# New call orders of four engines around the convolution of a hybrid decoder block, and nine convolution taps from GpSimd to VectorE

## What is computed

```
h = rmsnorm(x);  a_val, a_gate, b_in = split(h @ w_in)        # 512, 512, 512 channels
u  = a_val * sigmoid(a_gate)
ya = silu(layernorm(causal_dwconv(u, 31 taps) + bias))        # 4 channel groups of 128
yb = (sliding mean over 2, 4, 8, 16 tokens - token) @ pool_w * pool_scale
x  = x + concat(ya, yb) @ w_out
h  = rmsnorm(x);  gate, val = split(h @ w_up)                 # 2816 each
x  = x + (silu(causal_dwconv(gate, 3 taps)) * val) @ w_down
out = rmsnorm(x)
```

## Time and profile before

| | us |
|---|---|
| median of three runs | 907.63 |
| lowest, highest | 907.63, 907.78 |
| profiled execution, its span | 906.6 |
| busy: PE, PEld | 888.1, 735.1 |
| busy: DVE, POOL, ACT | 705.3, 674.6, 417.9 |

### The profile page before, as it was taken

How to read it: one execution, slowest core, us unless ns; L and a number is a source line. 1 busy time by engine, 2 the same in 40 slices (tenths; PEclk the granted TensorE clock), 3 DMA queues, 4 the chain that set the end, 5 groups by cost and what they waited for, 6 DMA issues and landing times.

```text
span 906.6 us, 11217 instructions
## 1 busy us (share of the span) xinstructions
PE 888.1 (98%) x4004; PEld 735.1 (81%) x4004; DVE 705.3 (78%) x759; ACT 417.9 (46%) x641; POOL 674.6 (74%) x505
## 2 busy tenths in 40 slices
PE   7999999899999999999999999999999999999996
PEld 6888887688888888888888888888888888888875
DVE  7799999997697895876858768587685876858667
ACT  8666656763564542433424434244342433424336
POOL 3679998683179896977959779597795977959822
PEclk9999999999999999999999999999999999999999
DMA  9221011151001112111121211312112021120114
GB/s 295 99 88 47 1 47 48 46 163 47 1 8 40 58 39 90 47 59 47 43 85 41 65 47 35 93 35 70 44 39 93 27 79 36 47 93 15 37 66 186
DMA packets 62997, 57.73 MB, mean 64 GB/s; under 512 B 2170, under 2 KB 56158, under 8 KB 62942
## 3 DMA queue, kind: packets, MB, share of 16 engines
q1 hardware_dynamic: 62942, 57.01, 20.0%
HBM read 52.81 MB, written 4.19 MB: 63 GB/s over the span
## 4 chain that ended last, share of the span: by engine, by line
PE 87%; DVE 7%; ACT 2%; issue 2%; DMA 1%; SPq 0%; POOL 0%; DVEq 0%; ACTq 0%; POOLq 0%
PE slot L2298 86%; DVE slot L1657 3%; PE slot L2330 1%; DVE w_lo L1622 1%; DMA x_sb<-in_x 1%; ACT junk L963 1%; DVE slot L1952 1%; DVE act_lo L1751 0%; DVE bn L1709 0%; DVE tokens L1698 0%; PE slot L2584 0%; ACT act_hi L972 0%; ACT std L966 0%; PE slot L2418 0%; PE slot L2406 0%
## 5 line engine op out<-in xcount | busy, mean ns | idle before, releaser
L753 POOL TENSOR_TENSOR ring<-raw,ring 128x512 fp32r<-128x512 f32 x200 | 275.3, 1395 | 106.2 <-ACT ring L1163 106.2
L1163 ACT ACTIVATE ring<-raw 128x512 fp32r<-128x512 f32 x204 | 120.7, 624 | 221.6 <-POOL raw L776 101.0
L2298 PE MATMUL slot<-act_hi,ring 128*128 128x512 f32 x680 | 219.7, 389 | 0.0
L1966 DVE TENSOR_TENSOR x_sb<-x_sb,slot 128x1024 f32<-128x1024 f32 x140 | 169.2, 1215 | 59.7 <-PE slot L2298 54.6
L2298 PE MATMUL slot<-sums,ring 128*128 128x512 f32 x780 | 186.9, 389 | 0.0
L2298 PEld LDWEIGHTS slot<-sums,ring 128*128 128x128 f32 x780 | 146.4, 188 | 30.4
L2298 PEld LDWEIGHTS slot<-act_hi,ring 128*128 128x128 f32 x680 | 127.7, 188 | 26.4
L715 POOL TENSOR_TENSOR conv<-conv,prod 128x512 f32<-128x512 f32 (+9 forms) x89 | 121.8, 1389 | 22.2 <-ACT prod L1078 15.5
L2298 PE MATMUL slot<-act_lo,ring 128*128 128x512 f32 x340 | 132.3, 389 | 0.0
L776 POOL TENSOR_TENSOR raw<-raw 128x512 f32<-128x512 f32 x88 | 121.6, 1383 | 13.0 <-POOL ring L753 3.4
L1657 DVE SCALAR_TENSOR_TENSOR slot<-x_sb,chan_head,slot 128x512 f32<-128x512 f32 (+16 forms) x143 | 102.0, 740 | 2.7
(11 more groups left out here) (201 smaller groups left out, 1462.8 us busy)
## 6 DMA issues: line engine op xcount, KB each, us to landing
raw<-in_w_up SPq DMA_DIRECT2D x44, 256.0 KB, 2.9
raw<-in_w_up SPq DMA_DIRECT2D x22, 512.0 KB, 3.8
raw<-in_w_down SPq DMA_DIRECT2D x22, 512.0 KB, 3.3
x_sb<-in_x SPq DMA_DIRECT2D x12, 512.0 KB, 6.1
raw<-in_w_in SPq DMA_DIRECT2D x4, 1024.0 KB, 5.0
raw<-in_w_out SPq DMA_DIRECT2D x4, 1024.0 KB, 4.9
out<-raw SPq DMA_DIRECT2D x7, 512.0 KB, 2.6
raw<-in_w_in SPq DMA_DIRECT2D x4, 512.0 KB, 8.6
```

The source lines that it names most:

```text
L753: nc.gpsimd.tensor_tensor(block_at(n, 1), block_raw(n), block_at(n, 0).bitcast(F32), ALU.subtract).then_inc(block_lo, 1)
L1163: nc.scalar.activation(block_at(n, 0), block_raw(n), ACT.Copy).then_inc(block_hi, 1)
L1966: nc.vector.tensor_tensor(dst, dst, slot[part_slot(i, p)][:, :].rearrange("p (a n) -> p a n", a=2), ALU.add).then_inc(part_added, 1)
L2298: mm = nc.tensor.matmul(out_ap, st[s], mv[v], start=first and s == v == 0, stop=last and s == 1, skip_group_check=onto)
```

## The change

Four call lists and the tables that belong to them are put in another order between the first taps and the loop over channel pairs, and the split of the taps (`LIGHT`) is set anew: (0,1) 20 to 19, (1,0) 11 to 9, (2,0) 11 to 8, (3,0) 10 to 7, (3,1) 14 to 13, (2,1) 14 to 15. The change is described as fifteen of GpSimd's taps given to VectorE; by this table ten are given and one is taken back, and GpSimd's number falls from 89 to 80. No instruction is new in kind. ScalarE's `sqrt_table()`, a one-element activation that brings in the table for the square root, is moved from ahead of `diff_hi(0)` to far behind.

```diff
-            ("pool", 0), ("pool", 1), ("pool", 2), ("pool", 3), ("out", 0), ("out", 1), ("t2", 0), ("t2", 1),
-            ("out", 2), ("out", 3), ("ln", 1, 0), ("ln", 1, 1), ("back", 1, 0), ("back", 1, 1), ("t2", 2), ("out", 4),
+            ("pool", 0), ("pool", 1), ("pool", 2), ("pool", 3), ("out", 0), ("out", 1), ("t2", 0), ("out", 2),
+            ("t2", 1), ("out", 3), ("ln", 1, 0), ("ln", 1, 1), ("back", 1, 0), ("back", 1, 1), ("t2", 2), ("out", 4),
...
-        LIGHT = {(0, 0): 5, (0, 1): 20, (1, 0): 11, (2, 0): 11, (1, 1): 12, (3, 0): 10, (2, 1): 14, (3, 1): 14}
+        LIGHT = {(0, 0): 5, (0, 1): 19, (1, 0): 9, (1, 1): 12, (2, 0): 8, (2, 1): 15, (3, 0): 7, (3, 1): 13}
...
             out(1, 0)
+            out(0, 1)
+            pool_product(2)
             out(1, 1)
-            pool_product(2)
-            out(0, 1)
             out(1, 2)
             pool_product(3)
             out(0, 2)
-            out(2, 1)
             out(0, 3)
             out(1, 3)
+            out(2, 1)
             out(2, 3)
-            out(3, 1)
             t2(0)
...
             join(2, 1)
             join(3, 1)
             t2_lo(1)
-            x1(2)
-            x1(3)
             ln_stat(1, 0)
             ln_stat(1, 1)
```

More of the change, by code:

```diff
@@ L1377, in _ @@
[L1377 to L1386 removed]
+            product(1, 1, 9)
+            product(3, 1, 2)
+            pool_tokens_half()
+            half_hi(6, 1)
+            product(3, 0, 5)
+            product(3, 1, 3)
+            product(2, 1, 3)
@@ L1387, in _ @@
+            product(3, 0, 6)
+            product(3, 1, 1)
+            half_hi(7, 0)
+            first_tap(3, 1)
             pool_tokens(2)
-            half_hi(7, 0)
-            product(2, 1, 3)
-            product(2, 1, 2)
             pool_tokens(1)
-            half_hi(7, 1)
-            sqrt_table()
             diff_hi(0)
             ln_std(0, 0)
+            half_hi(7, 1)
+            ln_std(0, 1)
             ln_z(0, 0)
-            ln_std(0, 1)
             ln_z(0, 1)
+            pool_tokens(0)
@@ L1399, in _ @@
             ln_z(0, 2)
             ln_z(0, 3)
-            pool_tokens(0)
+            diff_hi(1)
+            half_hi(8, 0)
             ln_silu(0, 0)
             ln_silu(0, 1)
-            diff_hi(1)
+            ln_silu(0, 2)
             pool_output(0)
-            ln_silu(0, 2)
+            product(2, 1, 5)
             ln_silu(0, 3)
+            pool_output(1)
             product(1, 1, 10)
-            half_hi(8, 0)
-            pool_output(1)
             diff_hi(2)
-            product(2, 1, 5)
@@ L1473, in _ @@
             s1_high(6)
+            high(0, T3)
+            sqrt_table()
+            s3_high(6)
             s2_high(5)
-            s3_high(6)
             p1_copy(0)
@@ L2031, in _ @@
             unit_lo(5, 0)
-            taps((2, 0, 5))
+            taps((2, 0, 4))
+            taps((1, 1, 2), (2, 0, 2))
+            taps((2, 0, 2))
+            tap(1, 1)
+            taps((2, 0, 4))
+            make_u(3)
             tap(1, 1)
             tap(2, 0)
-            taps((1, 1, 2))
-            tap(2, 0)
+            unit_lo(5, 1)
+            taps((2, 0, 3))
             tap(1, 1)
-            tap(2, 0)
-            make_u(3)
-            taps((2, 0, 7))
-            tap(1, 1)
-            taps((2, 0, 2))
-            tap(1, 1)
-            join(2, 0)
-            taps((3, 0, 3))
-            unit_lo(5, 1)
-            tap(3, 0)
-            tap(1, 1)
-            taps((3, 0, 7))
-            taps((1, 1, 2))
-            taps((3, 0, 3))
-            unit_lo(6, 0)
+            taps((2, 0, 4))
+            join(2, 0)
+            taps((3, 0, 2))
+            taps((1, 1, 2), (3, 0, 2))
+            taps((3, 0, 2))
+            unit_lo(6, 0)
+            taps((3, 0, 3))
+            taps((1, 1, 2), (3, 0, 2))
+            taps((3, 0, 7))
+            tap(1, 1)
             taps((3, 0, 2))
             tap(1, 1)
-            taps((3, 0, 2))
+            taps((3, 0, 4))
+            tap(1, 1)
+            join(3, 0)
+            pool_difference(3)
             unit_lo(6, 1)
-            tap(1, 1)
-            pool_difference(3)
-            taps((3, 0, 3))
-            join(3, 0)
-            taps((3, 1, 2))
-            unit_lo(7, 0)
             ln_stat(0, 0)
@@ L2066, in _ @@
             ln_stat(0, 2)
-            ln_shift(0, 0)
             ln_stat(0, 3)
             ln_aggr(0, 1)
+            tap(1, 1)
+            ln_shift(0, 0)
+            unit_lo(7, 0)
+            ln_shift(0, 1)
             tap(3, 1)
-            ln_shift(0, 1)
+            pool_difference(2)
+            unit_lo(7, 1)
             diff_lo(0)
-            unit_lo(7, 1)
-            tap(1, 1)
-            pool_difference(2)
             ya_lo(0, 0)
+            tap(3, 1)
             ya_lo(0, 1)
-            tap(1, 1)
-            tap(3, 1)
-            tap(1, 1)
             diff_lo(1)
@@ L2089, in _ @@
             unit_lo(8, 0)
+            diff_lo(3)
             unit_lo(8, 1)
-            diff_lo(3)
             tap(3, 1)
             yb_lo(2)
-            unit_lo(9, 0)
             join(1, 1)
             tap(3, 1)
+            tap(2, 1)
+            unit_lo(9, 0)
+            tap(2, 1)
+            yb_lo(3)
             unit_lo(9, 1)
-            yb_lo(3)
-            tap(2, 1)
-            taps((3, 1, 2))
-            tap(2, 1)
-            taps((3, 1, 2))
+            taps((2, 1, 2), (3, 1, 2))
             taps((2, 1, 2))
+            tap(3, 1)
             x1(0)
-            taps((2, 1, 2))
+            tap(3, 1)
             x1(1)
@@ L2109, in _ @@
             norm_apply(FFN, 0)
+            norm_apply(FFN, 1)
             tap(2, 1)
-            norm_apply(FFN, 1)
-            taps((2, 1, 3))
+            tap(3, 1)
+            taps((2, 1, 2))
+            taps((3, 1, 4))
+            tap(2, 1)
+            x1(2)
+            tap(2, 1)
+            tap(3, 1)
+            tap(2, 1)
             t2_lo(0)
@@ L2146, in _ @@
             s2_make(4)
+            x1(5)
             s3_low(4)
```

255 lines of the change are left out of this document (114 added, 141 removed), and 38 rows, old and new, of tables (ADDS, HI_PIECES, PRODUCTS).

## The result

| | before | after |
|---|---|---|
| median of seven runs on one chip, us | 907.78 (907.45 to 908.49) | 910.40 (908.86 to 911.52) |
| profiled execution, its span, us | 906.6 | 907.0 |
| busy PE, DVE, ACT, POOL, us | 888.1, 705.3, 417.9, 674.6 | 886.9, 702.1, 412.6, 657.2 |

The changed kernel is slower by the ratio 1.0025 (95% interval 1.0015 to 1.0034), 2.3 us; the forecast was 910.0. The two profiled spans show only 0.4 of it. The profiled run of after took 908.86, the shortest of its seven, while before's span with the 2.0 us that its runs have outside the span (1.8 for after) is 908.6, above its median. What sets the short runs of after apart is that no fall of the clock costs them anything, as the experiments show.

The account below looks back on a forecast made before the run. TensorE was taken as the bound, busy 888.1 of 906.6 us, with VectorE late at its waits. Terms 1.0 + 0.4 + 0 + 0.7 + 0.3 = +2.4 gave a 909.0 span, plus 1.0 for the median: 910.0 us, range 905.3 to 913.5.

Parts of the forecast that it names:

- signs of being wrong: Wrong if `out(0, 0)` starts before 161, the clock stays at 1, or VectorE reaches the second half's joins before 212.
- `pool_product(1)`, +1.0 and +0.4 for drawn-out subtractions: Second TensorE fence: start 1.0 us later through layer norm and silus, plus 0.4 for VectorE's drawn-out subtractions (-0.5 to +2.7).
- The table load, 0: ScalarE behind `diff_hi(0)`: a 1.28 us load now follows, counted at 0, or 1.3 if VectorE is faster than thought.
- The clock, 0 with bounds of 1.7: Around `pool_product(1)`: the fall to the lower clock costs the same 1.7 us as before, so 0, bounds -1.7 and +1.7.
- The rival of re-cut waits with the clock kept, 908.3: TensorE's two waits become four smaller ones and the clock keeps its full level: +0.7, 908.3 us; chance 0.17.
- `out(0, 3)`, +0.7: TensorE, directly behind `out(0, 2)`: waits for `unit_lo(9, 1)` behind `yb_lo(3)`, 3.4 us against one `out` of 2.77.
- The joins of the second half, +0.3: Last fence, `ln_tokens(1, 0)`: VectorE's added taps end these joins at 212 to 216 us; +0.3, bounds 0 and 2.
- VectorE's sum: Rival: second-half joins end near 217.5, `ln_tokens(1, 0)` comes 4 us late, 911.8 us; chance 0.17.
- GpSimd's relief is worth nothing: GpSimd's lighter load costed at nothing: it idles 32 us after its last add and TensorE does not wait for it.

Follow-up runs that it names:

- e6_sqrt_early: The changed kernel with the warm-up `sqrt_table()` ahead of `diff_hi(0)` again; 910.03 us, ratio 1.0016 to the kernel before.
- e1_again: The changed kernel once more, with no edit, for a second profile; 910.32 us, ratio 1.0021 to the kernel before.

## Why the prediction was right

The cost of the new order and the places where it is paid came out; some of the working beneath them did not, and its errors cancel in the sum. Two of the prediction's own signs of being wrong came true in the profiled run: its clock stayed at 1, and VectorE was at the first of the late joins at 211.75, before 212.

- **`pool_product(1)`, +1.0 and +0.4 for drawn-out subtractions.** Measured +1.12, counted from `ln_tokens(0, .)`. The start of `out(0, 0)`, forecast 163.3, was 163.28, but by two errors that cancel: the join came at 144.62, not 145.7, and the last `ln_z` ended at 155.87, not 156.8; then `diff_hi(1)` waited 0.62 us for `pool_difference(2)`, held up by `unit_lo(7, 0)`'s 2.32 us, and the pairs of silu and copy took 1.27 from start to start and 1.38 for the last.
- **The table load, 0.** Right, by little: `ln_std(0, 0)` at 150.87 was there just ahead of the shift at 151.26, and e6_sqrt_early won nothing by moving it. The Trainium skill's figure for a switch (ScalarE: Activation LUTs, What ACT_TABLE_LOAD costs), 2.66 us, is not what the path saw: `ln_std(0, 0)` starts 0.02 us behind the end of a load of 1.28.
- **The clock, 0 with bounds of 1.7.** Right for most runs, wrong for the profiled one. Forecast as a single outcome, it is an alternative from run to run: kept, lost in a wait at no cost (e1_again), or lost at `out(0, 0)` for 1.4 to 1.7 (e6_sqrt_early). Before pays 1.7 in both its profiles. This makes the two profiled spans nearly equal, and most of the spread of 2.7 us; the rest is other variation from run to run, as the 0.6 in the head of e6_sqrt_early. So the forecast of 909.0 for the profiled span was missed (907.0), while the median, 910.4, came near the forecast one, because 13 of 18 runs are long. That the median would stand 1.0 above the span was wrong as a rule too: a run's own time is 1.8 to 2.0 above its own span. The rival of re-cut waits with the clock kept, 908.3, describes the short runs (908.7 to 909.0).
- **`out(0, 3)`, +0.7.** Measured 1.03 of idle, and 1.27 of delay: TensorE's matmul ahead of the wait starts at 183.79 and the next at 185.21, 1.42 apart instead of 0.23, and the one behind it follows 0.31 later. The chain was named, but its pieces take 1.12 + 1.28 + 1.21 = 3.6 and the pauses between them, and the second chain into it, through `half_hi(9, 1)` behind `pool_output(3)`, was missed.
- **The joins of the second half, +0.3.** They ended at 213.5, ahead of TensorE at 214.35: 0. VectorE's sum did not bind: TensorE shows no wait there.
- **Sum.** Forecast +2.4 (1.4 + 0 + 0.7 + 0.3), measured +2.4 to `ln_tokens(1, 0)` at equal clock (1.12 + 1.27 + 0), 2.3 to 2.6 in the medians. So the first and the last term were too high by 0.3 each and `out(0, 3)` too low by 0.6: that the sum agrees to a tenth is luck, and the range of 905.3 to 913.5 held more than one outcome. That GpSimd's relief is worth nothing was right: its idle ahead of an add grew instead, waiting for ScalarE's products (12.0 us before and 28.5 after, from 50 to 212 us).

Left open: what decides in a run whether the clock is kept. No run here tells it, since runs of the same code differ.

## What to carry to other kernels

Compare two profiles from the last event that the change leaves in its place, and at equal clock: here the spans differed by 0.4 us, the code by 2.4 and the medians by 2.6. Where the engine that makes the operands is full, moving unhurried work behind one result puts it ahead of the next; add up all waits before and after, not the one that was attacked. A move on one engine is only as good as the producers of its inputs on the others: look up every wait of the moved instruction, not only those of its consumer.
